# Three matmuls of 256 columns into one accumulator range in place of one of 512 and one of 256

## The chip, the core and the metric

The kernel runs on one core of a Trainium2 chip. A core has five engines with an instruction queue each, which meet only through semaphores: TensorE (matrix products, from on-chip memory into the accumulator banks, PSUM), VectorE, ScalarE and GpSimd (elementwise work), and SyncE, which issues DMA transfers. The metric is the time of one execution on the device in microseconds (us); lower is better.

## What is computed

One layer of a hybrid streaming encoder for one sequence of 256 frames and 16 meta tokens, width 2048, all in float32. One input projection feeds eight retention heads and eight latent-attention heads; their outputs go through one output projection and a residual; then a squared-ReLU MLP of width 8192 with a residual, and a last norm.

```python
u = rmsnorm(h, norm_mix_g)
rq, rk, rv, rg, cq, ckv, kr = jnp.split(u @ w_in, IN_SPLITS, axis=-1)      # 2048 -> 4928
ret = retention_chunkwise(rope(rq), rope(rk), rv)
ret_out = jax.nn.silu(rg) * head_groupnorm(ret, ret_out_g)
q = rmsnorm(cq, q_norm_g) @ w_uq
o_lat = mla_attention(q_lat, q_rope, c_kv, k_rope, chunk_id, key_valid)
mla_out = rmsnorm(mla, mla_out_g)
h = h + jnp.concatenate([ret_out, mla_out], axis=-1) @ w_o                 # 2048 -> 2048
m = rmsnorm(h, norm_mlp_g)
h = h + jnp.square(jax.nn.relu(m @ w_up)) @ w_down                         # 2048 -> 8192 -> 2048
return rmsnorm(h[:, CHUNK:CHUNK + S], final_norm_g)
```

(The reference, shortened: reshapes and the latent products are left out.)

## The kernel before

Everything lies transposed: features on the 128 partitions, frames along the columns. A product of the large matrices is made in blocks of 128 output features; the weights of a block come as one chunk of 1 MB (16 tiles of 128x128, one per 128 input features), which SyncE loads into four buffers `raw`.

**Three products for one.** TensorE takes float32 in a reduced form (`F32R`). So each operand is split into a large part and a remainder: ScalarE rounds half a chunk into `hi` (`split_hi`), VectorE makes `lo = raw - hi` (`split_lo`), two buffers each. The moving side is split likewise: `xs` holds for each of 16 tiles the large part of 272 tokens and then the remainder, `hid` the large part of 256 frames and then the remainder. A block is the sum over its tiles of hi·large + hi·rest + lo·large.

**`wide` (lines 291 to 311)** is the block for the 256 frames. Per tile it does a matmul of 512 columns (weights `hi`, moving side large part and rest next to each other) into the whole bank `acc`, and one of 256 columns (weights `lo`, moving side the large part) into the bank's second half. So the first half gathers hi·large and the second the two others. The halves have to be added: ScalarE's `b_copy` (line 560) copies the second half into `half_b` once the block is done, and the engine that needs the block adds the two. VectorE's `sum_ab` (line 838) does so for the query latents, `zq`, `gate_z` and `z`; in the output projection and the down projection GpSimd's `res_sum` (line 1267) adds `half_b` to the residual, and VectorE's `residual` (line 1119) adds the first half to that. `mla_project` (line 341) does the same for the side products `ps_qn` and `ps_qr`, with copies `qn_b` and `qr_b`.

**`narrow` (lines 323 to 338)** is the block for all 272 tokens (keys, values): per tile three matmuls of 272 columns, all into the same columns, in the order lo·large, hi·rest, hi·large. Nothing is added afterwards.

**The order of the work** is written out by hand, per engine. TensorE: seven first blocks (0 to 6), then per head four blocks (gate of the head before, query, key, value) with the small products of attention and retention between them, the last gate block, 16 output blocks, and then twice 32 up blocks and 16 down blocks of two chunks each. While TensorE works on chunk c, ScalarE and VectorE split chunk c+2; a block uses one of two banks `acc`, and TensorE waits (`acc_read`) only for the block two before it to have been read. ScalarE's queue in a frame block is: first half of `split_hi`, `b_copy`, second half, and what follows from the block.

**The seam** between the last head and the output projection: VectorE scales the latent outputs (`mla_scale`), makes the remainders in `hid` (`mla_rest`, line 1087), reads the last gate block, and does the last head's norm; GpSimd scales four tiles, multiplies `gate_z` by the norm factor (`gate_norm`, line 1232) and by it `cen`. TensorE's first output block waits for the tiles one by one. SyncE loads the residual (`x_frames`) into `res` once the last gate is made (line 266), and GpSimd waits for it (`x_back`, line 1275).

**The tail**: after the last down block `b_copy`, `sum_ab` and an add, the square, the sum over features by TensorE (`ps_x`), root, reciprocal, scaling, and four stores.

## Time and profile before

| | |
|---|---|
| median of 3 runs | 1194.4 us (1194.34 to 1195.76) |
| span of the profiled execution | 1192.3 us |
| TensorE busy, matmuls | 1152.4 us, 6758 of them |
| TensorE busy, weight loads | 1004.7 us, 6758 of them |
| VectorE / ScalarE / GpSimd busy | 736.5 / 609.2 / 154.3 us |
| mean granted clock of TensorE | 0.986 of full speed |
| read from HBM | 203.84 MB |

The profile is of one execution, and its span is the time between the first and the last instruction; the runs' times are of other executions and take in what lies around the span, so a sum made within the profile is set against 1192.3 and not against 1194.4. Each matmul instruction comes with a weight load of its own, which runs beneath the matmul before it, in a row of its own. Matmuls are pipelined: the printed duration of one reaches into the next, and the pace is to be read from start to start.

### The profile page before, as it was taken

How to read it: one execution, taken by the hardware profiler on the slowest of the kernel's cores; microseconds unless marked ns; L12 is line 12 of the kernel's file. 1: busy time of each engine (PE TensorE's matmuls, PEld its weight loads, DVE VectorE, ACT ScalarE, POOL GpSimd, SP SyncE). 2: the span in 40 equal slices, each digit the busy share in tenths (PEclk: the TensorE clock that was granted, in tenths of full speed). 3: DMA queues.
4: the chain of work that ended last, by engine and by line, in shares of the span. 5: the costliest groups of instructions: out<-in, count | busy, mean ns of one | idle time of the engine just before them, and what ended most of it. 6: DMA issues, size and time to landing. Idle time of an engine off the chain costs nothing.

```text
span 1192.3 us, 18902 instructions
## 1 busy us (share of the span) xinstructions
PE 1152.4 (97%) x6758; PEld 1004.7 (84%) x6758; DVE 736.5 (62%) x962; ACT 609.2 (51%) x942; POOL 154.3 (13%) x167
## 2 busy tenths in 40 slices
PE   2999999999998999999999999999999999999995
PEld 2897898888887888888888888888888888888884
DVE  7786767677768667666665444445666665444443
ACT  4454565555556556555554444444555554444441
POOL 5011111111113331000000111111000000111111
PEclk7999999999999999999999999999999999999997
DMA  7443433333415554554555555455455445544531
GB/s 295 183 163 133 168 133 132 132 145 128 167 71 216 190 193 176 187 200 177 182 201 180 177 199 187 176 184 198 183 177 200 185 177 189 198 176 180 204 109 70
DMA packets 29260, 206.33 MB, mean 173 GB/s; under 512 B 3376, under 2 KB 3376, under 8 KB 5680
## 3 DMA queue, kind: packets, MB, share of 16 engines
q1 hardware_dynamic: 28080, 199.66, 46.4%
q10 hardware_dynamic: 1152, 6.29, 1.4%
q8 instruction: 18, 0.29, 0.1%
q14 instruction: 10, 0.08, 0.0%
HBM read 203.84 MB, written 2.10 MB: 173 GB/s over the span
## 4 chain that ended last, share of the span: by engine, by line
PE 95%; DVE 3%; ACT 1%; DMA 1%; issue 0%; DVEq 0%; SPq 0%; ACTq 0%
PE acc L289 86%; PE ps_qn L289 3%; PE ps_qr L289 2%; DVE xs L845 1%; PE ps_y L289 1%; PE ps_v L289 1%; PE ps_x L289 1%; PE ps_kn L289 1%; DMA x_in<-x_all 1%; DVE res L828 0%; DVE lo L828 0%; ACT xs L591 0%; DVE hid L1089 0%; DVE mla_o L828 0%; ACT hi L546 0%
## 5 line engine op out<-in xcount | busy, mean ns | idle before, releaser
L828 DVE TENSOR_TENSOR lo<-raw,hi 128x1024 fp32r<-128x1024 f32 x366 | 450.3, 1231 | 245.0 <-ACT hi L546 240.7
L289 PE MATMUL acc<-xs,hi 128*128 128x512 f32 (+1 forms) x1952 | 589.3, 365 | 0.0
L546 ACT ACTIVATE hi<-raw 128x1024 fp32r<-128x1024 f32 x366 | 386.6, 1057 | 234.5 <-PE acc L289 228.4
L289 PE MATMUL acc<-xs,lo 128*128 128x256 f32 (+1 forms) x1648 | 457.9, 286 | 22.2 <-DVE xs L845 22.2
L289 PE MATMUL acc<-hid,hi 128*128 128x512 f32 x1280 | 450.8, 400 | 3.2 <-DVE hid L1089 3.2
L289 PEld LDWEIGHTS acc<-xs,hi 128*128 128x128 f32 x1952 | 346.7, 190 | 51.6
L289 PE MATMUL acc<-hid,lo 128*128 128x256 f32 x1280 | 352.3, 281 | 0.0
L289 PEld LDWEIGHTS acc<-xs,lo 128*128 128x128 f32 x1648 | 312.3, 190 | 31.3 <-DVE lo L828 9.1
L289 PEld LDWEIGHTS acc<-hid,hi 128*128 128x128 f32 x1280 | 238.1, 189 | 59.5 <-DVE hid L1089 4.5
L289 PEld LDWEIGHTS acc<-hid,lo 128*128 128x128 f32 x1280 | 242.5, 189 | 4.7
L546 ACT ACTIVATE half_b<-acc 128x256 f32<-128x256 f32 x132 | 50.7, 384 | 216.7 <-PE acc L289 216.7
L1197 POOL TENSOR_TENSOR t<-half_b,res 128x256 f32<-128x256 f32 x47 | 34.7, 739 | 658.1 <-ACT half_b L546 650.3
L828 DVE TENSOR_TENSOR res<-acc,t 128x256 f32 (+1 forms) x47 | 20.0, 425 | 90.6 <-POOL t L1197 90.6
L828 DVE TENSOR_TENSOR z<-acc,half_b 128x256 f32<-128x256 f32 x64 | 27.2, 425 | 54.6 <-ACT half_b L546 54.6
L1197 POOL TENSOR_TENSOR sum_sq<-sum_sq,sq 128x256 f32<-128x256 f32 x47 | 51.8, 1102 | 56.1 <-ACT sq L810 36.8
L1148 DVE SCALAR_TENSOR_TENSOR r<-z,rstd 128x256 f32<-128x256 f32 x64 | 27.3, 426 | 2.2
L788 ACT ACTIVATE sq<-r 128x256 f32<-128x256 f32 x64 | 26.8, 418 | 3.3 <-DVE r L1148 3.1
L828 DVE TENSOR_TENSOR hid<-sq,hid 128x256 f32 (+1 forms) x64 | 26.9, 420 | 0.0
L789 ACT ACTIVATE hid<-r 128x256 f32 (+1 forms) x64 | 25.7, 402 | 0.0
L810 ACT ACTIVATE sq<-res 128x256 f32 (+1 forms) x32 | 13.5, 421 | 21.1 <-DVE res L828 21.1
L845 DVE SCALAR_TENSOR_TENSOR xs<-x_in,gains,xs 128x272 fp32r<-128x272 f32 x16 | 22.3, 1464 | 0.2 <-ACT xs L591 0.2
L1197 POOL TENSOR_TENSOR rk<-zk,consts 128x272 f32<-128x272 f32 x8 | 8.3, 1034 | 65.9 <-ACT swk L546 65.9
(175 smaller groups left out, 621.0 us busy)
## 6 DMA issues: line engine op xcount, KB each, us to landing
raw<-w_up SPq DMA_DIRECT2D x64, 1024.0 KB, 4.8
raw<-w_down SPq DMA_DIRECT2D x64, 1024.0 KB, 4.8
raw<-w_in SPq DMA_DIRECT2D x38, 1024.0 KB, 4.8
raw<-w_o SPq DMA_DIRECT2D x16, 1024.0 KB, 4.8
side<-w_side ACTq DMA_DIRECT2D x8, 768.0 KB, 5.8
x_in<-x_all SPq DMA_DIRECT2D x4, 544.0 KB, 7.7
res<-x_frames SPq DMA_DIRECT2D x1, 2048.0 KB, 7.6
out<-res SPq DMA_DIRECT2D x2, 640.0 KB, 3.0
```

Of the source, the lines that this page charges most:

```text
L289: return pe.matmul(o, l, m, start=start, stop=stop)
L546: return act.activation(o, i, ACT.Copy)
L788: act.activation(sq[:], r[:], ACT.Square).then_inc(sem["up_sq"], 1)
L789: act.activation(hid[:, n, 0:FRAMES], r[:], ACT.Square).then_inc(sem["up_hi"], 1)
L810: act.activation(sq[:], res[:, n, :], ACT.Square).then_inc(sem["dn_sq"], 1)
L828: return dve.tensor_tensor(o, a, b, op)
L845: dve.scalar_tensor_tensor(out=xs[:, k, TOK:], in0=x_in[:, k, :], scalar=gain(G_MIX + k), in1=xs[:, k, 0:TOK].bitcast(F32), op0=ALU.mult, ...
L1148: dve.scalar_tensor_tensor(out=r[:], in0=z[:], scalar=0.0, in1=rstd[:], op0=ALU.max, op1=ALU.mult).then_inc(sem["up_r"], 1)
L1197: return pool.tensor_tensor(o, a, b, op)
```

## The change

`wide` becomes `frames`: for each tile three matmuls of 256 columns, in the order of `narrow`, all into the first half of the bank. `mla_project` does the same for its two products. With that the block is complete in the bank:

- `b_copy`, `half_b`, `qn_b`, `qr_b` and their semaphores go.
- VectorE's `sum_ab` becomes `block_done`, a wait for the block's last matmul. Where a sum was, VectorE now copies (`cq`, `zq`, `qr_z`), multiplies by the norm factor in the same instruction (`qn`, `gate_z`; the second product, on VectorE for `qn` and on GpSimd for `gate_z`, goes), takes the ReLU and the factor straight from the bank (`r`), or adds the residual (`res`).
- GpSimd's `res_sum` and `gate_norm` go. The wait for `x_back` moves from GpSimd to VectorE, ahead of the loop over output blocks.
- ScalarE waits for `h_ss` and `dn_ss` before it writes `sq`, which GpSimd's running sum of the block before reads.

```diff
-            def wide(c, b, wide_of, hi_of, more=0, bmore=0, first=True, last=True, order=None, ready=None):
+            def frames(c, b, lo_of, hi_of, more=0, bmore=0, first=True, last=True, order=None, ready=None):
...
-                a = acc[b % 2]
+                a = acc[b % 2][:, 0:FRAMES]
...
                     wh = hi[c % 2][:, k * P:k * P + P]
                     wl = lo[c % 2][:, k * P:k * P + P]
-                    end = last and n == KT - 1
-                    if end:
-                        mm(a[:, FRAMES:], wl, hi_of(k), False, False)
-                    m = mm(a[:].rearrange("p (a t) -> p a t", a=2), wh, wide_of(k), first and n == 0, end)
-                    if not end:
-                        m = mm(a[:, FRAMES:], wl, hi_of(k), False, False)
+                    mm(a, wl, hi_of(k), first and n == 0, False)
+                    mm(a, wh, lo_of(k), False, False)
+                    m = mm(a, wh, hi_of(k), False, last and n == KT - 1)
...
-            def sum_ab(o, b, w, wmore=0):
-
-                dve.wait_ge(sem["half_b"], w + 1 + wmore)
-                return tt(o, acc[b % 2][:, 0:FRAMES], half_b[w % 2][:], ALU.add)
+            def block_done(c, b, more=0):
+
+                dve.wait_ge(sem["chunk_used"], 2 * c + 2 + 2 * more)
+                return acc[b % 2][:, 0:FRAMES]
...
-            def gate_sum(g, c, w, m, wm):
+            def gate_norm(g, c, m):
                 split_lo(c + 2, 0, m)
-                sum_ab(gate_z[:], c, w, wm).then_inc(sem["acc_read"], 1)
+                tt(gate_z[:], block_done(c, c, m), rstdx[:, META:], ALU.mult).then_inc(sem["acc_read"], 1)
                 split_lo(c + 2, 1, m)
...
-            def residual(n, b, res_ready):
-
-                dve.wait_ge(res_ready[0], res_ready[1])
-                tt(res[:, n, :], acc[b % 2][:, 0:FRAMES], t2[:], ALU.add).then_inc(sem["acc_read"], 1)
+            def residual(n, c, b, more):
+                tt(res[:, n, :], block_done(c, b, more), res[:, n, :], ALU.add).then_inc(sem["acc_read"], 1)
...
+            dve.wait_ge(sem["x_back"], 16)
             with dve.Fori(0, KT // 4) as i:
                 for j in range(4):
                     wo_block(4 * i + j, j, 4 * i)
```

How the instructions stand, on TensorE, at the end of the last down block (`hi_53` and `lo_55` are buffers of split weights). Before:

```order
L289 MATMUL acc<-hid,lo_55 128x256 x2
L289 MATMUL acc<-hid,hi_53 128x512
L532 REGISTER_ALU
L532 COMPARE_AND_BRANCH
L289 MATMUL ps_x<-sum_sq,consts 128x256
L289 MATMUL ps_x<-sq,consts 128x256
```

After:

```order
L269 MATMUL acc<-hid,lo_55 128x256
L269 MATMUL acc<-hid,hi_53 128x256 x2
L506 REGISTER_ALU
L506 COMPARE_AND_BRANCH
L269 MATMUL ps_x<-sum_sq,consts 128x256
L269 MATMUL ps_x<-sq,consts 128x256
```

Two instructions per tile have become three, the last two with the same weights; the sums over features behind them are as they were.

On VectorE, the last two down blocks and the tail (`t_70` is the tile `t2`). Before:

```order
L828 TENSOR_TENSOR lo_55<-raw_51,hi_53 128x1024
L828 TENSOR_TENSOR res<-acc,t_70 128x256
L828 TENSOR_TENSOR t_70<-acc,half_b_61 128x256
L828 TENSOR_TENSOR res<-t_70,res 128x256
L1186 RECIPROCAL rstd<-z 128x256
L828 TENSOR_TENSOR res<-res,rstd 128x256 x12
```

After:

```order
L784 TENSOR_TENSOR lo_55<-raw_51,hi_53 128x1024
L784 TENSOR_TENSOR res<-acc,res 128x256
L1131 RECIPROCAL rstd<-z 128x256
L784 TENSOR_TENSOR res<-res,rstd 128x256 x12
L83 UNCONDITIONAL_BRANCH
```

The last block's sum and add have become one add that reads the bank.

On GpSimd, the seam: the scaling of the latent outputs, the last gate, and the start of the output projection (`half_b_60` is the copy of the bank's second half). Before:

```order
L1197 TENSOR_TENSOR mla_o<-mla_o,rstd 128x256 x4
L1197 TENSOR_TENSOR gate_z<-gate_z,rstdx 128x256
L1197 TENSOR_TENSOR cen<-cen,gate_z 128x256
L1273 MEMSET sum_sq 128x256
L1276 UNCONDITIONAL_BRANCH
L1276 ISA
L1197 ISA
L1197 TENSOR_TENSOR t_70<-half_b_60,res 128x256
```

After:

```order
L1142 TENSOR_TENSOR mla_o<-mla_o,rstd 128x256 x4
L1142 TENSOR_TENSOR cen<-cen,gate_z 128x256
L1206 MEMSET sum_sq 128x256
L1208 UNCONDITIONAL_BRANCH
L1208 ISA
L1142 TENSOR_TENSOR sum_sq<-sum_sq,sq 128x256
```

The product that makes `gate_z` and the sum with the residual have gone from GpSimd's queue.

## Rows read from the trace of the kernel before

**Rows 1.** The page: busy us, share and count of each engine; granted clock, 40 slices.

```profile
PE 1152.4 (97%) x6758; PEld 1004.7 (84%) x6758; DVE 736.5 (62%) x962; ACT 609.2 (51%) x942; POOL 154.3 (13%) x167
...
PEclk7999999999999999999999999999999999999997
```

**Rows 2.** TensorE's waits in the whole span: us in total, times, longest.

```profile
PE acc L289 <- DVE xs L845: 22.2, 5, 9.2
PE acc L289 <- DVE hid L1089: 3.2, 3, 1.8
```

**Rows 3.** Groups of matmuls by shape: count, busy us, mean ns of one, idle before.

```profile
L289 PE MATMUL acc<-xs,hi 128*128 128x512 f32 x1344 | 471.1, 397 | 0.0
L289 PE MATMUL acc<-hid,hi 128*128 128x512 f32 x1280 | 450.8, 400 | 3.2 <-DVE hid L1089 3.2
```

**Rows 4.** Timeline of TensorE, starts of stages: start us, us, instruction, form, count.

```profile
816.84 0.39 PE L289 MATMUL acc<-xs,hi 128*128 128x512 f32 x1
...
996.25 0.39 PE L289 MATMUL acc<-hid,hi 128*128 128x512 f32 x1
...
1177.04 0.59 PE L289 MATMUL ps_x<-sum_sq,consts 128*128 128x256 f32 x2
```

**Rows 5.** The chain that ended last, one head: start us, us, what, matmuls.

```profile
110.91 5.60 PE acc L289 x32
...
119.78 6.02 PE acc L289 x48
...
140.87 1.40 PE ps_qr L289 x8
```

**Rows 6.** Timeline of TensorE in a down block.

```profile
1000.01 0.28 PE L289 MATMUL acc<-hid,lo 128*128 128x256 f32 x1
1000.13 0.40 PE L289 MATMUL acc<-hid,hi 128*128 128x512 f32 x1
1000.37 0.28 PE L289 MATMUL acc<-hid,lo 128*128 128x256 f32 x1
```

**Rows 7.** Busy us by stretch, narrow, then up: length, PE, PEld, DVE, ACT, POOL.

```profile
119.75:126.40 6.65, 6.65 (x56) 6.58 (x55) 3.38 (x9) 3.17 (x9) 0.00 (x0) 1.00 0.70 276
...
820.00:990.00 170.00, 170.00 (x973) 148.98 (x972) 110.04 (x151) 94.63 (x151) 0.74 (x2) 1.00 0.52 186
```

**Rows 8.** The chain that ended last, a transpose of 128 columns.

```profile
125.91 0.11 PE ps_kn L387
```

**Rows 9.** Timeline of the seam, VectorE, GpSimd and ScalarE.

```profile
362.76 1.63 POOL L1197 TENSOR_TENSOR gate_z<-gate_z,rstdx 128x256 f32<-128x256 f32 x1 [1.09 <-DVE gate_z L828]
...
363.74 1.81 DVE L1089 SCALAR_TENSOR_TENSOR hid<-mla_o,gains,hid 128x256 fp32r<-128x256 f32 x2
364.43 0.42 ACT L698 ACTIVATE gate<-gate_z 128x256 f32<-128x256 f32 x1 [1.15 <-POOL gate_z L1197]
...
368.28 1.27 DVE L1089 SCALAR_TENSOR_TENSOR hid<-mla_o,gains,hid 128x256 fp32r<-128x256 f32 x3
```

**Rows 10.** Stretches at the seam; the granted clock stands ahead of the DMA share.

```profile
368.00:370.00 2.00, 1.97 (x5) 1.54 (x6) 2.00 (x6) 1.36 (x2) 0.00 (x0) 0.50 0.98 418
370.00:372.00 2.00, 2.00 (x10) 1.73 (x9) 2.00 (x2) 0.41 (x2) 0.00 (x0) 0.70 0.98 418
```

**Rows 11.** Timeline of the tail, ScalarE and VectorE.

```profile
1177.24 0.38 ACT L546 ACTIVATE half_b<-acc 128x256 f32<-128x256 f32 x1 [8.78 <-PE acc L289]
...
1178.12 0.43 DVE L828 TENSOR_TENSOR res<-t,res 128x256 f32<-128x256 f32 x1
```

**Rows 12.** Load of the residual on the page; timeline after it: VectorE, GpSimd, ScalarE.

```profile
res<-x_frames SPq DMA_DIRECT2D x1, 2048.0 KB, 7.6
...
369.81 2.36 DVE L828 TENSOR_TENSOR lo<-raw,hi 128x1024 fp32r<-128x1024 f32 x2
...
373.33 0.73 POOL L1197 TENSOR_TENSOR t<-half_b,res 128x256 f32<-128x256 f32 x1 [7.82 <-DMA res<-x_frames]
...
377.24 0.38 ACT L546 ACTIVATE half_b<-acc 128x256 f32<-128x256 f32 x1 [0.72 <-PE acc L289]
```

More of the change, by code:

```diff
@@ L91 @@
 ret_o_ps ret_o cen_ps cen ret_sq var_ps ret_sd ret_inv ret_y ret_a ret_hi ret_lo
-gate_raw gate_z gate_exp gate_den gate_inv gate
-x_back wo_res h_ready m_hi m_lo h_sq h_ss h_ss_ps h_sd h_rstd
-up_z up_r up_sq up_hi up_lo dn_res dn_h dn_sq dn_ss fin_ps fin_sd fin_rstd fin_out fin_g fin_pool last_a stored
+gate_raw gate_exp gate_den gate_inv gate
+x_back h_ready m_hi m_lo h_sq h_ss h_ss_ps h_sd h_rstd
+ up_sq up_hi up_lo dn_h dn_sq dn_ss fin_ps fin_sd fin_rstd fin_out fin_g fin_pool stored
 side_landed first_half gains_landed consts_landed table_in""".split()
@@ L125, in hymba_block @@
         res = place("res", [KT, FRAMES])
-        half_b = [place(f"half_b{i}", [FRAMES]) for i in range(2)]
         gains = place("gains", [G_END])
@@ L450, in head @@
                 m = 4 * i
-                wide(c, c, x_wide, x_hi, m, m, ready=inside({6: lambda: mla_values(0)}) if first else None)
+                frames(c, c, x_rest, x_hi, m, m, ready=inside({6: lambda: mla_values(0)}) if first else None)
                 mla_project(h)
                 ret_scores(h - 1, first)
-                wide(c + 1, c + 1, x_wide, x_hi, m, m)
+                frames(c + 1, c + 1, x_rest, x_hi, m, m)
                 mla_scores(h)
@@ L655, in mla_in @@
             def mla_in(h):
-                act.wait_ge(sem["qn_ps"], h + 1)
-                copy(qn_b[:], ps_qn[:, FRAMES:]).then_inc(sem["qn_b"], 1)
-                act.wait_ge(sem["qr_ps"], h + 1)
-                copy(qr_b[:], ps_qr[:, FRAMES:]).then_inc(sem["qr_b"], 1)
                 act.wait_ge(sem["v_ps"], h + 1)
@@ L803, in down @@
                     if ahead:
-                        split_hi(c + 2, 0, more)
-                        split_hi(c + 2, 1, more)
-                    wide_block(c + 1, bd + j0, wd + j0, more, ahead)
+                        split_both(c + 2, more)
+                        split_both(c + 3, more)
                     act.wait_ge(sem["acc_read"], bd + n + 1)
-                    if half == 1 and not ahead:
-                        act.wait_ge(sem["dn_ss"], 2 * KT - 1)
+                    act.wait_ge(sem["dn_ss"], n + 1 + half * (KT + 1))
                     act.activation(sq[:], res[:, n, :], ACT.Square).then_inc(sem["dn_sq"], 1)
@@ L1167, in down @@
                         split_lo(c + 3, 0, m)
-                    if half == 1 and not ahead:
-                        sum_ab(t2[:], bd + j0, W_MLP + 2 * B_HALF - 1).then_inc(sem["last_a"], 1)
-                        dve.wait_ge(sem["last_a"], 1)
-                        tt(res[:, n, :], t2[:], res[:, n, :], ALU.add).then_inc(sem["acc_read"], 1)
-                    else:
-                        residual(n, bd + j0, (sem["dn_res"], n + 1 + half * KT))
+                    residual(n, c + 1, bd + j0, m)
                     if ahead:
@@ L1281, in _, with down @@
             for half in range(2):
[L1282 to L1287 removed]
+                pool.wait_ge(sem["h_ss_ps"] if half == 0 else sem["dn_ss"], 1 if half == 0 else KT + 1)
+                pool.memset(sum_sq[:], 0.0).then_inc(sem["dn_ss"], 1)
+                pool.wait_ge(sem["dn_ss"], half * (KT + 1) + 1)
+                def down(n, last=False):
                     if not last:
[L1289 removed]
                         pool.wait_ge(sem["dn_sq"], n + 1 + half * KT)
```

163 lines of the change are left out of this document (62 added, 101 removed).

## The prediction

> **What bounds the kernel now.** First the busy shares of the page: TensorE is busy 97% of 1192.3 us, VectorE 62%, ScalarE 51%, GpSimd 13%, and the granted clock is at 0.9 or more in all slices but the first and the last [rows 1]. Then TensorE's waits: 22.2 us for the input's split at the start, which the change doesn't touch, and 3.2 us for `hid` at the seam between the input projection and the output projection [rows 2]. There is no wait between blocks. So only two things can move the end: the time TensorE needs per step, and the few microseconds at the seam and at the tail.
>
> A step here is one 128x128 tile of weights against the frames: now a matmul of 512 columns and one of 256. There are 1344 such steps on `xs` (input projection and up) and 1280 on `hid` (output projection and down) [rows 3]. What one costs is read from whole stages, start to start, since the printed durations overlap. The second up stage runs from 816.84 to 996.25, 512 steps in 179.41 us: 350.4 ns each. The second down stage runs from 996.25 to 1177.04, 512 steps in 180.79 us: 353.1 ns [rows 4]. A `frames` block inside a head agrees: 32 matmuls in 5.60 us, 16 steps of 350 ns [rows 5].
>
> **The matmuls: 512+256 becomes 256+256+256.** The columns are the same, 768; one matmul and one weight load are added per step. The new form is in the trace already: `narrow` does three matmuls per tile into one range of 272 columns, in the order small weights, large weights, large weights. Its 48 matmuls take 6.02 us, 376.3 ns for 16 triples of 816 columns, with no visible price for adding to the same columns three times running or for loading the same weights twice [rows 5]. The new step has 48 columns less. Taken off at narrow's own 0.461 ns a column that leaves 354.2 ns; taken off at the array's full speed of one column per cycle at 2.4 GHz (20.0 ns) it leaves 356.3. I take 354.2, because the cost goes by the column in stages of both kinds: down has two matmuls a step and 353.1/768 = 0.460 ns a column, narrow has three and 0.461. Up is the odd one, with 0.456. The lower bound is that best rate for all: 350.4.
> - `xs`: 354.2 - 350.4 = +3.8 ns, times 1344 = +5.1 us (0 to +7.9).
> - `hid`: 354.2 - 353.1 = +1.1 ns, times 1280 = +1.4 us (-3.5 to +4.1).
> - The side products `ps_qn` and `ps_qr`: 8 matmuls in 1.40 us, 4 steps of 350 [rows 5]; 64 steps at +4.2 ns = +0.3 us (0 to +0.4).
>
> Together +6.8 us.
>
> Does the added weight load cost by itself? In the timeline a 256-column matmul is followed by the next after 0.12 us, and one of 512 after 0.24 [rows 6]; during those 0.12 us the weights of the next one are loaded. A transpose of 128 columns with its own load takes 0.11 us [rows 8], so the load has room beneath 0.118 (354.2/3), though little. The load row is busy 6.58 of 6.65 us in narrow, against 148.98 of 170 in up [rows 7]: it will look full everywhere afterwards. The Trainium skill ("TensorE: Matmul & The Clock Gate", LDWEIGHTS and Back-to-back issue gap) gives 107 ns for loading 128 columns, and says that spacing in a stream is set by load and matmul both; the 0.11 us of the transposes agrees. The same section puts a fixed 2.5 ns on every matmul. As an estimate from that page alone, 2.5 ns for each of the 2688 added matmuls would be +6.7 us in place of +6.8, with a larger part of it on `hid`.
>
> **The copies and sums that go.** Each frame block loses ScalarE's copy into `half_b`, and the residual blocks lose a GpSimd add. In the stages this is worth nothing: TensorE doesn't wait for any of it [rows 2]. The accumulators come free earlier, but a block waits for the one two before it, 5.6 us earlier. VectorE's sum becomes a copy, a multiply or an add of the same size, and `z` is no longer written.
>
> At the **tail** they are on the path. Before, ScalarE's copy starts at 1177.24 after the last matmul, the sum follows, and the add that makes `res` starts at 1178.12 [rows 11]. Now that add starts where the copy did: -0.88 us, rounded -0.9. The rest of the tail is unchanged.
>
> At the **seam** VectorE's queue is the path: the last waits of TensorE are for `hid` halves that it makes. GpSimd's `gate_z` product takes 1.63 us beside it, and VectorE's two `hid` instructions take 1.81 us in that time, where three take 1.27 later, with GpSimd quiet [rows 9]. The product goes; VectorE makes it while it reads the accumulator. ScalarE's exponential, which waited 1.15 us for it, comes earlier too [rows 9]. Two `hid` instructions alone are worth 0.85, so VectorE's queue moves up by 1.81 - 0.85, about 0.9 us, and TensorE's longest wait there (1.8) shrinks by as much: -0.9 us. The bounds: 0, if GpSimd's `cen` product, now earlier, disturbs VectorE in its place; and -2.5, if the shorter wait also saves the clock, which stands at 0.50 from 368 to 370 and at 0.70 to 372 and so costs 1.0 + 0.6 us after that wait [rows 10]. After the wait of 1.8 the next late thing is the same chain; nothing else is queued behind it.
>
> **Waits that are added.** VectorE waits for `x_back` ahead of its first output block; GpSimd did before. The load of `res` takes 7.6 us and GpSimd starts at 373.33. Behind VectorE's wait stands the `lo` half of the third output chunk, which it had finished at 372.17 (369.81 and 2.36). TensorE needs it after 377, when the second output block is done [rows 12]. About 1.2 us of delay in 4 us of room: nothing; without that room it would cost the 1.2. The load is issued after the gate product, which comes earlier. ScalarE's new waits (`h_ss`, `dn_ss`) guard `sq` against GpSimd's running sum of the block before, a block or more old: nothing, or some tenths at the seam.
>
> **The sum.** +6.8 - 0.9 - 0.9 = +5.0 us on a span of 1192.3, so 1197.3. The median of the runs is 1194.4, 2.1 above the span (what lies around it, and the spread); with the same 2.1 the forecast is **1199.4 us**. By the bounds: low -3.5 - 0.9 - 2.5 = -6.9, 1187.5; high 7.9 + 4.1 + 0.4 - 0.9 = +11.5, 1205.9.
>
> **Rivals.**
> - *The split of the long matmul is free or a gain.* All 256-column matmuls run at the best rate seen, 0.456 ns a column: `xs` +0, `hid` -3.5, ends -1.8: -5.3 us, 1189.1, and 1187.5 if the clock is saved at the seam. It decides below 352.3 ns a step, where the steps cost no more than the ends give. For it: the `hid` stage's 512-column matmul is no cheaper than two of 256 in rows 6 (0.24 against twice 0.12). Against it: narrow, the one row with three matmuls per tile, is at 0.461.
> - *The two cancel.* A step between 352.3 and 353.3 with the seam worth more: 1193 to 1196.5. For it: 1 ns a step is 2.6 us, more than any single term at the ends, and less than the difference between the stages.
> - *The load sets the pace.* If narrow's 125.4 ns per matmul is the load's pace and not the columns', the new step costs 376.3: +25.9 x 1344 + 23.2 x 1280 = +64.5 us, less 1.8: 1257. For it: narrow's load row is 99% busy. Against: the 0.12 us of a 256-column matmul and the 0.11 of the transposes, each with a load beneath it [rows 6, 8].
> - *The added waits reach TensorE* at the seam: +1.2 us on the forecast; it stays within the range.
>
> **Chances.** A measurement of this kernel tells about 0.2%, 2.4 us, from no change. The forecast case (353.3 to 356.3 ns a step) 0.70; free or a gain 0.14; cancelling 0.13; the load's pace 0.03. So slower by more than 0.2%: 0.73, the same 0.13, faster 0.14. The range that holds 8 in 10 leaves out the load's pace, the lower part of the gain case and the last bit above: 1191.5 to 1205.
>
> **What would show it.** In the profile of the changed kernel: 512 steps of up in 181.3 us (now 179.4) and of down in 181.3 (now 180.8); TensorE's loads x2688 more and near 99% busy in the stages; the wait for `hid` at the seam about 0.9 shorter, and the granted clock there either still at 0.50 or not; at the tail, `res` on VectorE straight after the last matmul. If the up stage stays at 179.4, the per-column argument is wrong and the first rival holds; if it is near 192, the load sets the pace. If both stages come out as forecast and the total doesn't, the error is at the seam.

## The result, and the profile after

The changed kernel takes 1211.4 us (median of 4 runs, 1210.75 to 1212.23) against 1194.9 us before: a ratio of 1.0139, with an interval from 1.0125 to 1.0152. It is 1.4% slower, about 16.5 us. The forecast was slower too, but with 1199.4 us, in a range up to 1205; the sign was right, the size too small by a factor of more than three.

The page first: TensorE is as busy as before in share, the row of its weight loads has gone from 84% to 95%, the other engines are down [rows 1].

```profile
PE 1171.2 (97%) x9446; PEld 1145.5 (95%) x9446; DVE 706.7 (58%) x889; ACT 556.7 (46%) x794; POOL 128.7 (11%) x112
```

TensorE's waits. None is new, and the three are as before or shorter [rows 2]; so the time isn't in a wait. Of the third, the first line here is the kernel before, the other three are the changed one:

```profile
PE ps_x L289 <- ACT sq L810: 1.4, 1, 1.4
...
PE acc L269 <- DVE xs L801: 21.4, 5, 9.3
PE acc L269 <- DVE hid L1043: 2.9, 2, 1.8
PE ps_x L269 <- ACT sq L766: 0.5, 1, 0.5
```

The timeline at the borders of the last two stages (start, duration, instruction), as in [rows 4]:

```profile
827.61 0.28 PE L269 MATMUL acc<-xs,lo 128*128 128x256 f32 x1
...
1010.22 0.28 PE L269 MATMUL acc<-hid,lo 128*128 128x256 f32 x1
...
1194.53 0.38 PE L269 MATMUL ps_x<-sum_sq,consts 128*128 128x256 f32 x1
```

The second up stage is 182.61 us long for 512 steps (before 179.41) and the second down stage 184.31 (before 180.79): 356.7 ns and 360.0 ns a step in place of 350.4 and 353.1. The chain of waits in a head, as in [rows 5]: the frame block 5.70 us in place of 5.60, the unchanged narrow block 6.02 as before.

```profile
112.05 5.70 PE acc L269 x48
...
121.03 6.02 PE acc L269 x48
```

In a down block the starts lie 0.12 us apart without exception, where [rows 6] alternated between 0.12 and 0.24 (the third row holds one, the second two matmuls):

```profile
1019.93 0.28 PE L269 MATMUL acc<-hid,lo 128*128 128x256 f32 x1
1020.05 0.40 PE L269 MATMUL acc<-hid,hi 128*128 128x256 f32 x2
1020.29 0.28 PE L269 MATMUL acc<-hid,lo 128*128 128x256 f32 x1
```

Busy time by stretch: length, matmuls, loads, VectorE, ScalarE, GpSimd. The loads of up and down now have no idle time left (before 148.98 of 170 in up, [rows 7]).

```profile
830.00:1000.00 170.00, 170.00 (x1433) 170.00 (x1432) 94.92 (x119) 81.37 (x119) 1.03 (x2) 1.00 0.52 185
1015.00:1185.00 170.00, 170.00 (x1419) 170.00 (x1418) 78.76 (x75) 73.03 (x89) 20.95 (x15) 1.00 0.46 166
```

Where the 16.7 us between the spans (1192.3 and 1209.0) lie, stage by stage from the same timelines:

| stretch | before | after | difference |
|---|---|---|---|
| to the first frame block | 39.7 | 40.8 | +1.1 |
| from there to the first output step | 320.1 | 321.9 | +1.9 |
| output projection, first up block | 102.3 | 103.5 | +1.2 |
| rest of first up, first down | 354.8 | 361.4 | +6.6 |
| second up, second down | 360.2 | 366.9 | +6.7 |
| tail | 15.3 | 14.5 | -0.8 |

(us, rounded one by one.) The first row isn't the change's: with the same matmuls in that stretch, its end lies between 39.7 and 41.4 us in the profiles of this study.

The tail, VectorE and ScalarE: the add stands straight behind the last matmul, the square 0.46 us behind the add's start. From the end of the last block to the square it is now one instruction in place of three [rows 11].

```profile
1194.72 0.42 DVE L784 TENSOR_TENSOR res<-acc,res 128x256 f32<-128x256 f32 x1 [9.20 <-PE acc L269]
1195.18 0.42 ACT L766 ACTIVATE sq<-res 128x256 f32<-128x256 f32 x1 [10.21 <-DVE res L784]
```

### The profile page after: what moved, and what is told of

Same layout as the page of the kernel before. It is cut to its first block, busy times and chain, and to the rows that moved or that the text cites. A ratio compares the mean times of both kernels' runs of the same rounds, so it can differ in the third digit from the quotient of the medians.

```text
span 1209.0 us, 23868 instructions
## 1 busy us (share of the span) xinstructions
PE 1171.2 (97%) x9446; PEld 1145.5 (95%) x9446; DVE 706.7 (58%) x889; ACT 556.7 (46%) x794; POOL 128.7 (11%) x112
## 4 chain that ended last, share of the span: by engine, by line
PE 95%; DVE 3%; ACT 1%; DMA 1%; issue 0%; DVEq 0%; SPq 0%; ACTq 0%
PE acc L269 86%; PE ps_qn L269 3%; PE ps_qr L269 2%; DVE xs L801 1%; PE ps_y L269 1%; PE ps_v L269 1%; PE ps_x L269 1%; PE ps_kn L269 1%; DMA x_in<-x_all 1%; DVE res L784 0%; DVE lo L784 0%; ACT xs L554 0%; DVE mla_o L784 0%; DVE hid L1043 0%; ACT hi L520 0%
## 5 line engine op out<-in xcount | busy, mean ns | idle before, releaser
L269 PE MATMUL acc<-xs,hi 128*128 128x256 f32 (+1 forms) x3296 | 600.3, 286 | 0.0
L269 PEld LDWEIGHTS acc<-xs,hi 128*128 128x128 f32 x3296 | 511.6, 190 | 0.7
L269 PE MATMUL acc<-xs,lo 128*128 128x256 f32 (+1 forms) x1648 | 473.4, 287 | 21.4 <-DVE xs L801 21.4
L269 PE MATMUL acc<-hid,hi 128*128 128x256 f32 x2560 | 462.1, 283 | 0.0
L269 PEld LDWEIGHTS acc<-hid,hi 128*128 128x128 f32 x2560 | 400.3, 192 | 0.0
L1142 POOL TENSOR_TENSOR sum_sq<-sum_sq,sq 128x256 f32<-128x256 f32 x47 | 68.7, 1462 | 745.9 <-ACT sq L766 673.2
L1099 DVE SCALAR_TENSOR_TENSOR r<-acc,rstd 128x256 f32<-128x256 f32 x64 | 27.2, 425 | 32.8 <-PE acc L269 32.8
L784 DVE TENSOR_TENSOR res<-acc,res 128x256 f32 (+1 forms) x48 | 20.4, 425 | 39.4 <-PE acc L269 39.4
L1081 DVE SCALAR_TENSOR_TENSOR xs<-res,gains,xs x16 | 15.2, 947 | 0.2 <-issue 0.2
L784 DVE TENSOR_TENSOR side_lo<-side,side_hi 128x1280 fp32r<-128x1280 f32 x8 | 11.9, 1486 | 3.4 <-ACT side_hi L520 3.4
```

Of the source, the lines that this page charges most:

```text
L269: return pe.matmul(o, l, m, start=start, stop=stop)
L784: return dve.tensor_tensor(o, a, b, op)
L1081: dve.scalar_tensor_tensor(out=xs[:, j, TOK + META:], in0=res[:, j, :], scalar=gain(G_MLP + j), in1=xs[:, j, META:TOK].bitcast(F32), op0=A ...
L1099: dve.scalar_tensor_tensor(out=r[:], in0=block_done(c0 + j0, b0 + j0, m), scalar=0.0, in1=rstd[:], op0=ALU.max, op1=ALU.mult).then_inc(sem ...
L1142: return pool.tensor_tensor(o, a, b, op)
```

## The experiments

Every experiment is set against the second up and the second down stage, which are 512 steps each on `xs` and on `hid`, start to start; they hold no wait, and a stage has the same length in all profiles of the same matmuls (179.41 and 180.80 us in the kernel before and in e3, and 179.41 in the up stage of e9). The whole time goes with it. e5 to e8 and e10 to e15 are one run each. e3 to e8 and e11 to e15 leave products out and e10 takes other columns, so these are for the time alone. In brackets: matmuls a step in nearly all steps, and columns of weights they load.

| kernel | time, us | up, us | down, us |
|---|---|---|---|
| before (2; 128+128) | 1194.9 to 1195.5 | 179.41 | 180.80 |
| changed (3; 128+128+128) | 1211.4 | 182.62 | 184.30 |
| e1, before with the long one split (3; 3 x 128) | 1208.7 | 181.78 | 183.79 |
| e2, changed, other order (3; 3 x 128) | 1209.3 | 182.04 | 184.31 |
| e3, changed, old matmuls (2; 128+128) | 1194.3 | 179.41 | 180.80 |
| e4, changed (3; 128+64+64) | 1198.8 | 180.90 | 181.12 |
| e8, changed (3; 128+32+32) | 1196.0 | 179.63 | 181.27 |
| e14, changed (3; 32+32+32) | 1188.7 | 179.17 | 178.44 |
| e11, before, light weights under 512 columns (2; 32+128) | 1187.2 | 178.78 | 177.35 |
| e12, before, light weights under 256 columns (2; 128+32) | 1189.1 | 178.12 | 179.20 |
| e13, before (2; 32+32) | 1187.2 | 180.27 | 176.53 |
| e15, before, 384 and 384 columns (2; 128+128) | 1186.8 | 179.41 | 177.61 |

### The two parts apart: e1_split_apart and e3_old_matmuls

e1 is the kernel before with this edit in `wide`, for all steps but a chunk's first (a chunk is 16) and a block's last:

```diff
-                    if end:
+                    if end or n == 0:
...
+                    else:
                         mm(a[:, FRAMES:], wl, hi_of(k), False, False)
-                    m = mm(a[:].rearrange("p (a t) -> p a t", a=2), wh, wide_of(k), first and n == 0, end)
-                    if not end:
-                        m = mm(a[:, FRAMES:], wl, hi_of(k), False, False)
+                        mm(a[:, FRAMES:], wh, wide_of(k)[:, 1], False, False)
+                        m = mm(a[:, 0:FRAMES], wh, hi_of(k), False, False)
```

> The kernel before, with one edit on TensorE: in every step but the first and the last of a block the matmul of 512 columns is split into two of 256, which still write the two separate halves of the bank. ScalarE's copies and all sums stay. Theory A (each matmul instruction costs a fixed piece beside its columns, wherever it writes): 2360 of 2624 steps get one matmul more, +6.3 to 6.9 ns each by the stages of the changed kernel, so +15.6 us: about 1210.5 us, down stage about 183.8 us for 512 steps. Theory B (adding three times running to the same 256 columns is slow): the halves are still written as before, so the time stays at 1195 (within 2 us). Theory C (the copies and sums that went had hidden something on other engines): 1195 as well.

Measured: 1208.7 us, 1.011 of before (1.0093 to 1.0127). The timeline at the stages' borders:

```profile
826.07 0.40 PE L289 MATMUL acc<-xs,hi 128*128 128x512 f32 x1
...
1007.85 0.39 PE L289 MATMUL acc<-hid,hi 128*128 128x512 f32 x1
...
1191.64 0.38 PE L289 MATMUL ps_x<-sum_sq,consts 128*128 128x256 f32 x1
```

Up 181.78, down 183.79 us (the table). 448 of the 512 up steps and 464 of the 512 down steps are split (in the whole kernel 2328, by the 9086 matmuls against 6758, where the expectation had 2360), so a split costs 2.37 us / 448 = 5.3 ns and 2.99 / 464 = 6.4 ns, most of the changed kernel's 6.3 and 6.8. The order of the three is the changed kernel's. So are the steps away from a chunk's ends: on `xs` they alternate between 351 and 363 ns in both kernels, and on `hid` they are 360 ns in the changed kernel and 360 on average in e1. Every second step on `xs`, in e1 and then in the changed kernel, is 0.71 us behind the last:

```profile
832.47 0.28 PE L289 MATMUL acc<-xs,lo 128*128 128x256 f32 x1
...
833.18 0.28 PE L289 MATMUL acc<-xs,lo 128*128 128x256 f32 x1
...
833.89 0.28 PE L289 MATMUL acc<-xs,lo 128*128 128x256 f32 x1
```

```profile
833.32 0.28 PE L269 MATMUL acc<-xs,lo 128*128 128x256 f32 x1
...
834.03 0.28 PE L269 MATMUL acc<-xs,lo 128*128 128x256 f32 x1
...
834.74 0.28 PE L269 MATMUL acc<-xs,lo 128*128 128x256 f32 x1
```

What e1 is cheaper by lies in the unsplit steps and in those around them. Theories B and C fall: writing to the same columns costs nothing, and the copies and sums hide nothing. The split of the 512-column matmul is the cause.

e3 is the changed kernel with the old matmuls in `frames` (`mla_project` keeps its three, 64 matmuls more than before in all):

```diff
-                a = acc[b % 2][:, 0:FRAMES]
+                a = acc[b % 2]
...
-                    mm(a, wl, hi_of(k), first and n == 0, False)
-                    mm(a, wh, lo_of(k), False, False)
-                    m = mm(a, wh, hi_of(k), False, last and n == KT - 1)
+                    end = last and n == KT - 1
+                    both = lo_of(k)
+                    if end:
+                        mm(a[:, FRAMES:], wl, hi_of(k), False, False)
+                    m = mm(a[:].rearrange("p (a t) -> p a t", a=2), wh, both, first and n == 0, end)
+                    if not end:
+                        m = mm(a[:, FRAMES:], wl, hi_of(k), False, False)
```

> The other part alone: the changed kernel's ScalarE, VectorE and GpSimd (no copy, no sum), with the matmuls of before in the blocks (512 columns into the whole bank and 256 into its second half). The second half is never added, so the output lacks those two products; it is there for the time. Theory A: the step is back at 350.4 and 353.1 ns; the tail and the seam keep their gain of 0.8 and 0.5 us: 1193.6 us. Theory C (the slowdown comes with the other engines' new order, not with the matmuls): 1205 or more.

Measured: 1194.3 us, 0.9989 of before (0.9979 to 0.9998). The stages are back to the hundredth:

```profile
817.96 0.39 PE L269 MATMUL acc<-xs,hi 128*128 128x512 f32 x1
...
997.37 0.39 PE L269 MATMUL acc<-hid,hi 128*128 128x512 f32 x1
...
1178.17 0.38 PE L269 MATMUL ps_x<-sum_sq,consts 128*128 128x256 f32 x1
```

So all of the loss comes with the matmuls. What the elementwise part is worth is 0.02 to 0.2% of the time (0.2 to 2.5 us), which holds the 1.3 to 1.5 us that the forecast's tail and seam terms would give by their measured sizes (below), and the 1.8 of the forecast too.

### The order: e2_alternate

```diff
-                    mm(a, wl, hi_of(k), first and n == 0, False)
-                    mm(a, wh, lo_of(k), False, False)
+                    mm(a, wh, lo_of(k), first and n == 0, False)
+                    mm(a, wl, hi_of(k), False, False)
```

> The changed kernel with the three matmuls of a step in the order large weights x rest, small weights x large, large weights x large: no two loads in a row within a step bring the same weights. Theory A (fixed piece per matmul): 1211.4, within 1 us, 120 ns per matmul in the down stage. Rival (loading the same weights twice running is what costs): the extra 6.9 ns of a step go, 1195 to 1200, and the gap after the second matmul of a step falls.

Measured: 1209.3 us (2 runs), the down stage the same 184.31, up 182.04. The same weights twice running aren't what costs. On `xs` the order moves 0.6 us per stage, on `hid` nothing.

### How fast a full load can follow another: e5_cols240, e6_cols192, e7_cols128

The changed kernel with fewer columns of frames in all steps but a chunk's first, here with 192:

```diff
-                    mm(a, wl, hi_of(k), first and n == 0, False)
-                    mm(a, wh, lo_of(k), False, False)
-                    m = mm(a, wh, hi_of(k), False, last and n == KT - 1)
+                    t = 192 if n else FRAMES
+                    mm(a[:, 0:t], wl, hi_of(k)[:, 0:t], first and n == 0, False)
+                    mm(a[:, 0:t], wh, lo_of(k)[:, 0:t], False, False)
+                    m = mm(a[:, 0:t], wh, hi_of(k)[:, 0:t], False, last and n == KT - 1)
```

> The changed kernel, where every step of a block but the first multiplies only 240 of the 256 frame columns (16 columns of those products are missing in the output). Theory E, worked out from the runs so far: a matmul takes 17/16 of a cycle per column of frames, and each weight load adds 1/8 of a cycle per column of weights to the stream, though it runs beneath it (at 2.4 GHz: 256 columns 288 cycles, 120.0 ns; with 64 weight columns 280). Here 271 cycles, 112.9 ns per matmul, the down stage 174.1 us for 512 steps. Theory A (fixed piece, columns at one cycle): 113.3 ns, 174.7 us. Rival D (a full load takes 120 ns, whatever the columns): 120 ns, 184.3 us.

> The same with 192 of 256 columns. Theory E without a floor: 220 cycles, 91.7 ns, the down stage 143.5 us. A floor set by the load (the transposes of 128 columns start 110 ns apart): 107 to 112 ns, the down stage 166 to 173 us.

> The same with 128 of 256 columns. Theory E without a floor: 152 cycles, 63.3 ns, the down stage 103 us (unless VectorE's splitting becomes the bound, at about 2.7 us per chunk of 16 steps, 86 us). With a floor set by the load: the same spacing as with 192 columns, and the down stage of the same length; then the load's pace is measured: this spacing.

Measured: with 240 columns the down stage takes 172.80 us, with 192 columns 172.17 us. The first is lower than the three expectations (174.1, 174.7 and 184.3, so theory E's rule and theory A both miss by more than 1 us, and rival D, a load of 120 ns, falls), the second is on the floor that the load was to set (166 to 173). The borders of the last stage with 192 columns:

```profile
795.42 0.30 PE L269 MATMUL acc<-xs,lo 128*128 128x256 f32 x1
...
967.59 0.30 PE L269 MATMUL acc<-hid,lo 128*128 128x256 f32 x1
...
1139.76 0.40 PE L269 MATMUL ps_x<-sum_sq,consts 128*128 128x256 f32 x1
```

A stage is 512 x 3 = 1536 matmuls, so 172.17 us is 112.1 ns each, with each chunk's first step, of 256 columns, in it. Sixteen columns fewer than 256 save 7.5 ns a matmul, forty-eight more save 0.4: below some 240 columns a matmul with a full load doesn't get shorter. So a load of 128 columns can be repeated every 112 ns. The Trainium skill ("TensorE: Matmul & The Clock Gate", LDWEIGHTS) gives 107 ns for it; the trace has 5 ns more.

With 128 columns the whole time is no guide, 1850.2 us, because the clock went. But the frame blocks inside the heads still run at full clock (1.00 in that stretch), and there the floor shows: 48 matmuls take 5.33 us with 128 columns (the first line, e7) and 5.36 with 192 (the second, e6), 111.0 and 111.7 ns each. A third fewer columns save less than 1 ns.

```profile
110.45 5.33 PE acc L269 x48
```

```profile
110.60 5.36 PE acc L269 x48
```

The page of e7, two starts in its first down stage, and stretches at the seam (the granted clock stands ahead of the DMA share); then one stretch of e6:

```profile
PE 1809.8 (98%) x9446; PEld 1783.2 (96%) x9446; DVE 706.2 (38%) x889; ACT 556.1 (30%) x794; POOL 128.2 (7%) x112
...
PEclk8999999955555555555555555555555555555555
...
999.65 0.41 PE L269 MATMUL acc<-hid,hi 128*128 128x128 f32 x1
999.87 0.41 PE L269 MATMUL acc<-hid,lo 128*128 128x128 f32 x1
...
358.00:360.00 2.00, 2.00 (x20) 1.99 (x18) 2.00 (x5) 1.87 (x3) 0.91 (x2) 1.00 0.00 0
360.00:362.00 2.00, 0.72 (x6) 0.58 (x5) 2.00 (x3) 1.99 (x6) 1.66 (x2) 0.88 0.00 0
...
372.00:374.00 2.00, 2.00 (x12) 2.00 (x11) 0.83 (x2) 0.70 (x2) 0.74 (x1) 0.50 0.78 266
```

```profile
372.00:374.00 2.00, 2.00 (x19) 2.00 (x19) 0.91 (x3) 1.14 (x2) 0.78 (x1) 1.00 0.98 307
```

What the engine did before the clock fell: at the seam it waited for `hid`, busy 0.72 of 2.00 us. The clock falls there in the other kernels too [rows 10], and with 192 columns it is back at 1.00 from 372 us on (0.985 as the mean of the run). With 128 columns it stays at 0.50 to the end, although TensorE is busy without a gap. So what is lost with 128 columns is the return of the clock; inside the heads the same matmuls kept it. The starts are 0.21 us apart, and the last stage is 327.68 us for 1536: 213.3 ns, which is 256 cycles at 1.2 GHz, where one cycle a column would be 106.7 (the matmuls of 272 columns at half clock at the start, from 20 us on, are 227 ns apart: 272 cycles). The load sets that pace.

### How much of the added cost is the load: e4_half_weights, e8_quarter_weights, e13_two_light, e14_three_light

e4 and e8 shorten the two loads of the large weights in the changed kernel (64 and 32 columns of 128; `h` is 128 in a chunk's first and last step):

```diff
-                    mm(a, wh, lo_of(k), False, False)
-                    m = mm(a, wh, hi_of(k), False, last and n == KT - 1)
+                    mm(a[0:h, :], wh[:, 0:h], lo_of(k), False, False)
+                    m = mm(a[0:h, :], wh[:, 0:h], hi_of(k), False, last and n == KT - 1)
```

> The changed kernel, where in all steps of a block but the first and the last the two matmuls with the large weights take only 64 of the 128 weight columns (and write 64 partitions); the moving side keeps its 256 columns. The output lacks half of those products. Theory A in its plain form (a fixed piece per matmul that doesn't depend on the load): 120 ns per matmul, 1211. Rival D (the weight load is the pace: 128 columns of weights take as long as 256 columns of frames): two of three loads are half as long, so those gaps fall to about 107 to 112 ns, the down stage from 184.3 to 171 to 176 us, the whole to 1185 to 1195.

> The changed kernel, where in all steps of a block but the first and the last the two matmuls with the large weights take only 32 of the 128 weight columns (half of them in the earlier run); three quarters of those products are missing in the output. Theory E (the delay goes with the columns of weights loaded): a step of 840 cycles, 350.0 ns, the down stage 179.8 us (181.1 with 64 weight columns, 184.3 with 128). Theory A with a threshold (only a load longer than 64 columns disturbs, the rest is fixed per matmul): 181.1 as with 64.

Measured: down 181.12 and 181.27 us, up 180.90 and 179.63. With two of their three loads light, the three matmuls cost about what the two with full loads cost before (from 0.2 to 1.5 us a stage more).

Theory A in its plain form falls: the fixed piece does depend on the load. Rival D, which puts the whole pace on the load (171 to 176 us in e4), falls as well. Theory A with a threshold at 64 columns met e8 on `hid` (181.1 expected), but on `xs` e8 still gains 1.27 us over e4. Theory E, a price by the column of weights, met e4 (181.1) and missed e8 on `hid` (179.8 expected, 181.27 measured, no gain from 64 to 32). Its whole-step form for full loads (17/16 of a cycle per column of frames and 16 cycles per load) gives 288 cycles or 120.0 ns a matmul on `hid` and 848 cycles or 353.3 ns for a step before, as measured; but it was made from those rows, and it isn't a law for lighter ones.

e13 and e14 take all loads light, in the kernel before and in the changed one (`h` is 32 in all steps but a chunk's first and last):

```diff
+                    h = 32 if 0 < n < KT - 1 else P
...
-                    m = mm(a[:].rearrange("p (a t) -> p a t", a=2), wh, wide_of(k), first and n == 0, end)
+                    m = mm(a[0:h].rearrange("p (a t) -> p a t", a=2), wh[:, 0:h], wide_of(k), first and n == 0, end)
-                        m = mm(a[:, FRAMES:], wl, hi_of(k), False, False)
+                        m = mm(a[0:h, FRAMES:], wl[:, 0:h], hi_of(k), False, False)
```

> The kernel before, where in all steps of a block but the first and the last both matmuls (512 and 256 columns) take only 32 of 128 weight columns: the loads are nearly gone, the columns of frames stay 768. Three quarters of the products are missing in the output. If loads are what is paid above the columns, the step is at most the 340 ns seen with one light load, and the down stage about 175 us (180.8 with full loads, 177.4 and 179.2 with one of the two light).

> The changed kernel with all three matmuls of those steps at 32 weight columns. Theory L (the added load is what costs, the added matmul is free): stages as long as those of e13, within 0.5 us, about 175. Theory I (a matmul costs about 3 ns or more by itself): both stages at least 1.3 us longer than those of e13; with the whole 6.9 ns, 3.1 us longer.

The borders of e13, then of e14:

```profile
813.25 0.40 PE L289 MATMUL acc<-xs,hi 128*128 128x512 f32 x1
...
993.51 0.39 PE L289 MATMUL acc<-hid,hi 128*128 128x512 f32 x1
...
1170.04 0.38 PE L289 MATMUL ps_x<-sum_sq,consts 128*128 128x256 f32 x1
```

```profile
814.87 0.28 PE L269 MATMUL acc<-xs,lo 128*128 128x256 f32 x1
...
994.04 0.28 PE L269 MATMUL acc<-hid,lo 128*128 128x256 f32 x1
...
1172.48 0.38 PE L269 MATMUL ps_x<-sum_sq,consts 128*128 128x256 f32 x1
```

On `hid` the split costs 178.44 - 176.53 = 1.91 us with light loads, and 184.30 - 180.80 = 3.50 with full ones. On `xs` the split with light loads costs nothing (179.17 against 180.27, a gain), and 3.21 with full ones. And the two light loads on `xs` are slower than the two full ones (180.27 against 179.41), which no theory here foresaw.

The 1.91 us isn't a price of the added matmul either, for it is the mean of two cases. A down block is two chunks, the first on tiles 0 to 15 of `hid` and the second on 16 to 31. In e14 the first takes 5.49 us and the second 5.67, and so through the whole stage:

```profile
1005.18 0.28 PE L269 MATMUL acc<-hid,lo 128*128 128x256 f32 x1
...
1010.67 0.28 PE L269 MATMUL acc<-hid,lo 128*128 128x256 f32 x1
...
1016.34 0.28 PE L269 MATMUL acc<-hid,lo 128*128 128x256 f32 x1
```

Away from the chunk's ends a step is 340.0 ns in the first chunk and 353.3 in the second. In e13 it is 343.3 in both, and in the changed kernel 360.0 in both. So with light loads the same split gains 3.3 ns a step on one half of `hid` and costs 10.0 on the other. The two chunks also use different weight buffers; those alternate on `xs` as well, where e14's chunks are equal (5.60 us), so the buffers alone don't do it. Theory L (stages within 0.5 us) fails on `hid`; theory I (1.3 us or more in both) is met on `hid` by the mean and fails on `xs`. A load's price isn't a sum of single prices, and what the matmul costs without its load isn't shown.

### Where a load stands: e11_light_host, e12_light_short, e15_even

e11 shortens only the weights of the 512-column matmul (their load runs beneath the short matmul ahead), e12 only those of the 256-column one; the edits are the two lines of e13 apart. e15 shares out the columns as 384 and 384, with full loads:

```diff
-                    m = mm(a[:].rearrange("p (a t) -> p a t", a=2), wh, wide_of(k), first and n == 0, end)
-                    if not end:
-                        m = mm(a[:, FRAMES:], wl, hi_of(k), False, False)
+                    both = a[:].rearrange("p (a t) -> p a t", a=2)
+                    if end or n == 0:
...
+                    else:
+                        mm(both[:, :, 0:192], wh, wide_of(k)[:, :, 0:192], False, False)
+                        m = mm(both[:, :, 64:256], wl, wide_of(k)[:, :, 64:256], False, False)
```

> The kernel before, where in all steps of a block but the first and the last the matmul of 512 columns takes only 32 of the 128 columns of its weights. That load runs beneath the short matmul of the step before. Theory F: a full load (128 columns, 111.6 ns by the runs with fewer columns) beneath a matmul of 256 columns (118 ns) delays by 3.2 to 3.5 ns, a short load or one beneath 512 columns doesn't. So each step loses that: down stage 180.8 - 0.875 x 512 x 3.45 ns = 179.3 us, up stage 179.4 - 1.4 = 178.0. Theory A (a fixed piece per matmul): 180.8 and 179.4, unchanged.

> The counterpart: the kernel before, where the matmul of 256 columns takes only 32 of the 128 columns of the small weights. That load runs beneath the matmul of 512 columns. Theory F: nothing gained, 180.8 and 179.4 us. If loads delay by their size wherever they run (theory E), both this and the run before gain the same, 16 x 0.75 = 12 cycles or 5 ns a step: 178.6 and 177.2 us.

> The kernel before, where in all steps of a block but the first and the last the 768 columns are shared out as 384 and 384 in place of 512 and 256, with full loads (the first matmul leaves out 64 columns of each half, the second adds columns of the rest in their place; the output lacks and gains products). If a full load costs only beneath a short matmul (118 ns against the load's 111.6), no load costs here: the step falls to 340 to 347 ns, the down stage to 175 to 178 us. If it goes by the number of loads, nothing changes: 180.8 and 179.4.

Measured: e11 down 177.35 (-3.45), up 178.78 (-0.63); e12 down 179.20 (-1.60), up 178.12 (-1.29); e15 down 177.61 (-3.19), up 179.41 (0.00). On `hid` a full load costs more beneath the short matmul than beneath the long one (3.45 against 1.60), and the even split, in which no matmul is short, saves as much as a light load there (it met its 175 to 178 us). That is the way of theory F; but its sizes fail (1.5 and 0 expected), and theory E, with 2.2 us for each, fails too. On `xs` nothing of it holds: e11 saves less than e12, and e15 nothing. Nor does it hold on all of `hid`: e11's first chunks take 5.62 us and its second 5.47, where e12's are 5.60 in both and those of before 5.65. So where the load stands matters in one half of `hid` only, and theory F isn't shown.

### Does the place of the data matter: e10_from_zero

```diff
-                return xs[:, k, TOK + META:]
+                return xs[:, k, TOK:TOK + FRAMES]
...
-                return xs[:, k, META:TOK]
+                return xs[:, k, 0:FRAMES]
```

> The changed kernel, where the frame blocks on the input side read the tile's columns from 0 (the 16 meta columns and 240 frames) in place of from 16 on: other data, same sizes. It asks what makes a step on xs (356.7 ns) cheaper than one on hid (360.0). If it is where the moving columns start, the second up stage moves from 182.6 us by more than 0.3; if it is the distance between tiles (544 against 512 columns) or something else, it stays at 182.6, and the down stage at 184.3 in any case.

Measured: 1209.1 us in place of 1211.4, up 181.76 in place of 182.62, down 184.31, unchanged. So where the moving columns start moves a step on `xs` by 1.7 ns. It doesn't explain that `hid` is dearer; it goes the other way. The distance between tiles wasn't tried.

### A version that keeps the gain without the loss: e9_joined_at_ends

The kernel before, with `joined=True` in two calls: the last gate block, and the last down block (unrolled from its loop). There it does the three matmuls of 256, and the copy and the sum are gone:

```diff
+                    if joined:
+                        mm(a[:, 0:FRAMES], wl, hi_of(k), first and n == 0, False)
+                        mm(a[:, 0:FRAMES], wh, wide_of(k)[:, 1], False, False)
+                        m = mm(a[:, 0:FRAMES], wh, hi_of(k), False, end)
+                    else:
...
```

> The kernel before, with the three matmuls of 256 only where the sum of the halves stood on the path: in the last down block (32 steps) and in the last gate block (16 steps); everywhere else 512 and 256 with copy and sum. The tail gains 0.8 us and the seam about 0.5, as in the changed kernel; the 48 steps cost 0.3 us: about -1.0 us, 1194.4 against 1195.4. If the gain at the ends in the changed kernel came from somewhere else, no change.

Measured: 1194.5 us (11 runs) against 1195.3 (15 runs), 0.9993 (0.9984 to 1.0002). The medians differ by the expected amount, but the interval holds 1: not told from no change. Its second down stage is 0.22 us longer than before (32 steps at 6.9 ns).

## Why the forecast was wrong

- **What bounds it: right.** No wait was added that TensorE meets, no stage has another bound, and the time went with the step.
- **The price of a step: the step that failed.** It was put at 354.2 ns, between 350.4 and 356.3; it is 356.7 on `xs` and 360.0 on `hid`, above the upper bound in both. The terms: `xs` +6.3 ns x 1344 = +8.5 us where +5.1 was forecast, `hid` +6.9 x 1280 = +8.8 where +1.4 was forecast, against a sum of 16.7. Two errors are in it. First, narrow's price was scaled down in proportion to the columns. Its 376.3 ns became 356.7 with 48 columns less, 19.6 ns, so not even the full 20.0 of the upper bound went; the price above the columns isn't proportional to them. e6 shows the end of that line, where columns save almost nothing. Second, the row was of `xs` and was carried over to `hid`, though the forecast's own rows had `hid` 2.7 ns a step dearer. 356.7 + 2.7 would have been 359.4. The bound was made from one tile and held, within 0.4 ns, for that tile alone.
- **"The cost goes by the column in stages of both kinds": wrong.** 0.460 in down and 0.461 in narrow agreed because two differences cancelled: `hid` is dearer, and two matmuls are cheaper than three. Set against `xs` in up, with 0.456, narrow had shown a price for the third matmul: 376.3 x 768/816 - 350.4 = 3.8 ns. The forecast used that for `xs` and stopped there.
- **The load beneath the matmul: half wrong.** "Room, though little" was right in that the pace (112 ns) stays below the step's third (120). At full clock a load with 128 columns above it takes 111.0 ns (e7, in the heads). But room isn't the same as free: e4 and e8 give back 3.0 to 3.2 us of a down stage by making loads lighter. The rival "the load sets the pace" had the right culprit in part, and the wrong price (+64.5 us).
- **The Trainium skill's 2.5 ns for each added matmul** ("TensorE: Matmul & The Clock Gate", Back-to-back issue gap), by the forecast's estimate +6.7 us in place of +16.7, is no better than the sum. The measured price is 6.3 to 6.9 ns for a matmul with its load; for the matmul alone the runs give none (e14: from -3.3 to +10.0 ns a step on `hid`, by the tiles).
- **Copies and sums worth nothing in the stages: right**, shown by e3, whose stages are those of before.
- **The tail: right.** -0.9 forecast, -0.8 measured.
- **The seam: the right sign, smaller, and not by the wait it named.** -0.9 forecast, with TensorE's longest wait of 1.8 us shrinking by as much; it stayed at 1.8, and the waits for `hid` together went from 3.2 to 2.9. VectorE's two `hid` instructions on the path take 0.5 us less. The output projection with the first up block is 0.7 us shorter than its steps alone would make it (256 x 6.9 ns and 16 x 6.3 ns are 1.9, and it grew by 1.2); e2 and e10, with the same work on the other engines, have the output projection 0.1 and 0.4 us longer than the changed kernel, so the last tenths of this aren't told. The timeline there, with the row that answers for the third output chunk last:

```profile
365.72 1.64 POOL L1142 TENSOR_TENSOR cen<-cen,gate_z 128x256 f32<-128x256 f32 x1 [1.09 <-DVE gate_z L784]
...
366.25 0.42 ACT L657 ACTIVATE gate<-gate_z 128x256 f32<-128x256 f32 x1
...
366.70 1.34 DVE L1043 SCALAR_TENSOR_TENSOR hid<-mla_o,gains,hid 128x256 fp32r<-128x256 f32 x2
...
375.26 1.22 DVE L784 TENSOR_TENSOR lo<-raw,hi 128x1024 fp32r<-128x1024 f32 x1 [1.74 <-ACT hi L520]
```

VectorE's two `hid` instructions take 1.34 us in place of 1.81 [rows 9], but GpSimd's `cen` product, now earlier, takes 1.64 where the removed product took 1.63: the disturber has been replaced, as the bound of 0 had it, and half of the gain is there all the same. ScalarE's exponential has no wait any more. The clock still falls, later by two microseconds and as deep [rows 10]:

```profile
370.00:372.00 2.00, 1.49 (x6) 1.41 (x7) 2.00 (x7) 1.11 (x2) 0.00 (x0) 0.55 0.99 418
372.00:374.00 2.00, 2.00 (x13) 2.00 (x13) 1.51 (x3) 0.25 (x1) 0.00 (x0) 0.59 0.93 397
```

- **The added wait for `x_back`: right.** The `lo` half behind it starts at 375.26, and what it waits for is ScalarE's `hi`, not the load [rows 12].
- **The rivals.** "Free or a gain" and "the two cancel" fell at once by the stages. The range ended at 1205 because its upper end was made of the same two bounds.

What stays open: why a step on `hid` is dearer than on `xs`, why the price of light loads has the other sign on `xs` and on half of `hid`, and what exactly in a load delays the stream. The starts fall into patterns that repeat every few steps and move with the place of the data (e10, e14), the order (e2) and the mix of lengths (e15). Away from the chunks' ends (steps 4 to 15) the mean step of 768 columns on `hid` is 340.0, 343.3, 346.7, 350.0, 353.3 or 360.0 ns in all runs but e11, levels 3.3 ns or a multiple of it apart, which is 8 cycles at 2.4 GHz: the price comes in jumps. Addresses in the on-chip memory may be behind it; no run settles that.

## What to carry to other kernels

Count the matmuls and the loads, not the columns alone: here one more matmul of 256 columns with its full load in each step, at equal columns, cost 6.3 to 6.9 ns a step, and 2624 such steps outweighed everything that was saved on engines that nobody waited for. When a new form's price is taken from a row of another tile or length, take the difference of those tiles in rows of the same form first, and let the range reach past a bound that comes from one row. A sum that stands on the path only at the ends is worth changing only at the ends, if it can be measured at all. And before a stage's mean is taken for the price of an instruction, look at its chunks one by one: e14's mean was made of a gain and a loss.

## What the runs showed of the hardware

- A full load of 128 weight columns can follow the last every 111 to 112 ns at 2.4 GHz (e6; e7 in the heads) and every 213.3 ns at 1.2 GHz (e7); a matmul of 192 columns with such a load is no faster than one of 240 (112.1 against 112.5 ns).
- TensorE's granted clock fell to half where it waited at the seam; in the stream of 128-column matmuls with full loads that followed it never came back, at 98% busy by its own row (e7). At 192 columns it was back at 1.00 from 372 us on (e6).
- Columns being equal (768 a step), the time of a step ran from 344.8 to 360.0 ns on `hid` and from 347.9 to 356.7 on `xs`, depending on how the columns are shared out and how large the weights are.
- The same three matmuls with light loads took 340.0 ns a step on one half of `hid` and 353.3 on the other (e14).
- Adding into the same accumulator columns three times running costs nothing against writing two separate halves: the steps are 351 and 363 ns in turn on `xs` either way (e1).
